# Second chunk's and sample rows' embedding products at experts 20 to 22 instead of before and in experts 0 and 1

## The reference

```
x1 = LN1(alpha*x + W_out [pool_group(x) | mlstm_group(x)])
x2 = LN2(alpha*x1 + MoE(x1))            # top 4 of 32 experts, clamped SwiGLU
y  = x2 + sigmoid(x2 W_pg) * (p W_ple)  # gated per-layer input embedding
```

## Time and profile before

| | |
|---|---|
| median of 3 runs | 1104.46 us (1104.17 to 1105.55) |
| profiled execution | 1105.6 us, its span 1103.8 us |
| PE busy | 1077.7 us (98%), 5616 instructions |
| DVE busy | 436.8 us (40%) |
| ACT busy | 159.5 us (14%) |
| DMA | 440.69 MB, mean 399 GB/s |

### The profile page before, as it was taken

One profiled execution on the slowest core, in us unless ns is written; L12 is line 12 of the kernel. 1 busy time (PEld: TensorE's weight loads), 2 busy tenths in 40 slices (PEclk: granted clock), 3 DMA queues, 4 the chain that ended last, 5 costly groups with the idle time before them and its releaser, 6 DMA issues.

```text
span 1103.8 us, 14800 instructions
## 1 busy us (share of the span) xinstructions
PE 1077.7 (98%) x5616; PEld 425.9 (39%) x5616; DVE 436.8 (40%) x1109; ACT 159.5 (14%) x306; POOL 78.9 (7%) x107
## 2 busy tenths in 40 slices
PE   9999999999999999999999999999999999999998
PEld 7786433333333333333333333333333333333344
DVE  1648663333333333333333333333333333333345
ACT  1532341100000000000000000000000000000033
POOL 0747420000000000000000000000000000000000
PEclk9999999999999999999999999999999999999999
DMA  9989989999999999999999999999999999999961
GB/s 319 267 313 399 287 352 395 428 436 428 429 432 435 423 433 433 433 427 435 433 429 432 433 433 427 432 433 433 428 433 435 426 431 433 432 423 428 425 243 40
DMA packets 41027, 440.69 MB, mean 399 GB/s; under 512 B 8816, under 2 KB 16236, under 8 KB 25653
## 3 DMA queue, kind: packets, MB, share of 16 engines
q1 hardware_dynamic: 39945, 439.00, 95.4%
q0 software_dynamic: 368, 0.57, 0.2%
q10 hardware_dynamic: 676, 0.59, 0.2%
HBM read 436.61 MB, written 3.77 MB: 399 GB/s over the span
## 4 chain that ended last, share of the span: by engine, by line
PE 65%; DMA 20%; DVE 9%; issue 2%; POOL 2%; ACT 1%; DVEq 0%; SPq 0%; ACTq 0%; POOLq 0%
PE bank L1024 27%; DMA ring<-in_w_mlp 19%; PE bank L1104 16%; PE bank L971 4%; PE bank L605 3%; DVE proj L1663 3%; PE bank L1184 3%; PE bank L784 3%; DVE proj L1660 2%; DVE proj L1658 2%; PE bank L1085 1%; PE bank L984 1%; POOL ring L2141 1%; PE bank L1019 1%; PE bank L977 1%
## 5 line engine op out<-in xcount | busy, mean ns | idle before, releaser
L1024 PE MATMUL bank<-ring,proj 128*64 128x512 f32 x2024 | 461.5, 597 | 9.0 <-DMA ring<-in_w_mlp 9.0
L1624 DVE SCALAR_TENSOR_TENSOR xT<-bank,proj,xT 128x512 f32<-128x512 f32 x128 | 90.2, 746 | 428.3 <-PE bank L971 427.1
L1024 PEld LDWEIGHTS bank<-ring,proj 128*64 128x64 f32 x2024 | 137.6, 136 | 288.9 <-issue 263.0
L1104 PE MATMUL bank<-ring,pool_side 128*64 128x512 f32 x1024 | 226.8, 595 | 0.4 <-ACT pool_side L1993 0.4
L1104 PEld LDWEIGHTS bank<-ring,pool_side 128*64 128x64 f32 x1024 | 71.7, 137 | 133.3 <-issue 130.4
L1987 ACT ACTIVATE proj<-proj 128x256 f32<-128x256 f32 x64 | 26.7, 417 | 527.5 <-DVE proj L1657 527.5
L1615 DVE TENSOR_SCALAR proj<-bank,ln_rows_of_fours 128x64 f32<-128x64 f32 x256 | 67.4, 335 | 24.8 <-PE bank L984 24.8
L971 PE MATMUL bank<-mixT 64*128 64x512 f32 x264 | 74.5, 641 | 0.5 <-ACT mixT L1996 0.5
L605 PE MATMUL bank<-xT,ring 128*128 128x264 f32 x320 | 74.3, 388 | 0.3 <-ACT proj L1809 0.3
L605 PEld LDWEIGHTS bank<-xT,ring 128*128 128x128 f32 x320 | 59.9, 190 | 12.3 <-issue 1.6
L950 PE MATMUL bank<-xreg,proj 128*64 128x512 f32 x248 | 58.5, 592 | 0.0
(11 more groups left out here) (371 smaller groups left out, 634.6 us busy)
## 6 DMA issues: line engine op xcount, KB each, us to landing
ring<-in_w_mlp SPq DMA_DIRECT2D x77, 4096.0 KB, 27.6
ring<-in_w_mlp SPq DMA_DIRECT2D x36, 2048.0 KB, 14.9
ring<-in_w_in SPq DMA_DIRECT2D x9, 1024.0 KB, 14.9
ring<-in_w_out SPq DMA_DIRECT2D x4, 1024.0 KB, 8.8
ring<-in_w_ple_gate SPq DMA_DIRECT2D x4, 1024.0 KB, 26.9
xreg<-in_x_prompt SPq DMA_DIRECT2D x4, 512.0 KB, 4.1
ring<-q_row SPq DMA_DIRECT2D x1, 2048.0 KB, 7.0
ring<-k_row SPq DMA_DIRECT2D x1, 2048.0 KB, 7.3
```

Of the source, the lines that this page charges most:

```text
L1024: last = pe.matmul(first_bank(t, q), xgT[:, k % 4, k // 4, :], first_columns(rows_, t, q), start=False, stop=(k == KD - 1))
L1104: last = pe.matmul(bank[4][BLOCK * h:BLOCK * (h + 1), :], aT[:, m, BLOCK * t:BLOCK * (t + 1)], w[:, k % 2, 512 * h:512 * h + 512], start=F ...
L1624: ins = STT(total[:, c, s], ins_bank[h][:, :], gate_table[:, c, bass.ds(n, 1)], total[:, c, s], ALU.mult, ALU.add)
```

## The change

Half 0 of chunk 1's embedding moves to expert 20, half 1 to expert 21 (k = 0 behind the product k = 1, k = 1 behind the product k = 3), the sample rows' to expert 22 (behind k = 5). Both halves now use bank 3. In the two places before expert 0 where half 0 was computed, PE does `keep_dense(4)` and `keep_dense(2)` on bank 7. Experts 20 to 23 are written out on PE (`middle`); ACT's loop ends before expert 20. `late[1]` is no longer filled by SP: ACT issues this DMA in expert 22, behind its copy of the sample rows' embedding and ahead of that expert's sigmoid.

```diff
-        EMBED_BANKS = {0: (bank[1], bank[6]), 1: (bank[7], bank[3]), 2: (bank[5],)}
+        EMBED_BANKS = {0: (bank[1], bank[6]), 1: (bank[3], bank[3]), 2: (bank[5],)}
...
                 load_next(n)
-                if n == SLOTS + 18:
-                    sp.wait_ge(sem("ple_ps"), 3)
-                    load_late(1)
...
-            def keep_dense(times):
+            def keep_dense(times, unread=bank[2]):
                 for _ in range(times):
-                    pe.matmul(bank[2][:, 0:P], ident, ident, start=True, stop=True)
+                    pe.matmul(unread[:, 0:P], ident, ident, start=True, stop=True)
...
             count_places(1, ()).then_inc(sem("pos_ps"), 1)
-            pe.wait_ge(sem("ple_in"), 16)
-            early_embedding(0, (0,))
+            keep_dense(4, bank[7])
...
-                    if opening and j == 0 and k in (1, 3):
-                        early_embedding(1, (k // 2,))
-                    if opening and j == 0 and k == 1:
-                        pe.wait_ge(sem("ple_done"), 1)
+                    if middle and j < 2 and k in (1, 3):
+                        if (j, k) == (0, 1):
+                            pe.wait_ge(sem("ple_in"), 16)
+                        early_embedding(j, (k // 2,))
...
-                        if opening and j == 1:
-                            pe.wait_ge(sem("hotT_done"), 2)
+                        if middle and j == 2:
+                            pe.wait_ge(sem("hotT_done"), n + 1)
                             early_samples()
-                if opening and j < 2:
-                    pe.wait_ge(sem("ple_done"), j + 2)
+                if middle and j < 3:
+                    pe.wait_ge(sem("ple_done"), j + 1)
...
             spread_places(0)
-            early_embedding(0, (1,))
+            keep_dense(2, bank[7])
...
-            with pe.Fori(STEP, npass * EXPERTS - 2 * STEP, STEP) as n:
+            with pe.Fori(STEP, npass * EXPERTS - 3 * STEP, STEP) as n:
                 for j in range(STEP):
                     expert(n + j, j)
+            for j in range(STEP):
+                expert(npass * EXPERTS - 3 * STEP + j, j, middle=True)
...
-            embedded_early(0)
             act.nop().then_inc(sem("out_done"), 1)
...
-            for j in range(STEP):
-                if j == 0:
-                    embedded_early(1)
-                elif j == 1:
+            with act.Fori(0, npass * EXPERTS - 3 * STEP, STEP) as n:
+                for j in range(STEP):
+                    expert(n + j, j)
+            for j in range(2 * STEP):
+                if j < 2:
+                    embedded_early(j)
+                elif j == 2:
                     act.wait_ge(sem("ple_ps"), 3)
                     act.copy(embedded_samples, EMBED_BANKS[2][0][:, 0:256]).then_inc(sem("ple_done"), 1)
-                expert(j, j)
-            with act.Fori(STEP, npass * EXPERTS - STEP, STEP) as n:
-                for j in range(STEP):
-                    expert(n + j, j)
+                    act.dma_start(late[1], unit_weights(EXPERTS - 2 * STEP, 1)).then_inc(sem("late_in"), 16)
+                expert(npass * EXPERTS - 3 * STEP + j, j % STEP)
```

More of the change, by code:

```diff
@@ L1009, in first_bank, with expert @@
                 return bank[q][BLOCK * t:BLOCK * (t + 1), :].rearrange("p (x i) -> p x i", i=8)
-            def expert(n, j, closing=0, opening=False):
+            def expert(n, j, closing=0, opening=False, middle=False):
                 i4 = n - j
```

## The result

| | median | range | runs |
|---|---|---|---|
| before | 1104.95 us | 1104.17 to 1105.55 | 9 |
| after | 1108.22 us | 1105.41 to 1110.94 | 9 |

The ratio is 1.003, 95% interval 1.0021 to 1.0038: 3.3 us slower, outside the forecast range of 1102.8 to 1106.5 us, and slower by more than the 0.2% that the prediction set as the border of no change. Eight of the nine runs after have a mean granted clock of 0.997 or 0.998 of full speed; the ninth has 1.000, and took 1105.41 us. The profiled execution took 1108.37 us, its span 1106.6 us, mean clock 0.998.

A forecast was written before the change was run, and what follows sets the result against it. Loads set the pace, with 1.16 us of PE cover at expert 29's k = 4 quad. Stream -0.1, holes 0, late[1] 0, middle products 0: profiled 1105.6 becomes 1105.5, median 1104.4 us, range 1102.8 to 1106.5.

The forecast's parts named there:

- Clock (slower, 0.07): Rival, chance 0.07: clock falls to 1.2 GHz behind expert 0's new hole; stream moves 3.6 us, time 1108.0.
- The hole: Expert 0 without its two product pairs: PE waits 2.3 us for DVE before the second combine; their 2.1 us return nothing.
- The load that stood at 175.29: Load behind expert 0's second layer, last held back by slot release: the stream shifts with it, 0.1 us earlier.
- late[1] 0 (moved inside the same stream): Loads behind its early place come 2.43 us sooner; sent at about 791 it takes 2.43 us back: 0 in the sum.
- 0 to 1.5 us, if a part of the sixteen engines runs dry: Bounds for holes in the stream, closest at the first quad (landed 250.2), with late[1] no longer early; 0 taken.
- Written-out code: The new middle experts are written out, as those that gave PE's 27.99 us per expert; the sum has no term for it.
- The start's shift: Before expert 0, keep_dense(4) takes 1.28 us where early_embedding took 0.96: gather_chunk(1) starts 0.32 us later.
- The middle: Experts 20 to 22: the 5.2 us of products are swallowed, 2.4 by the earlier stream, 3.4 by slower loads; cost 0.
- The ring: Sign: the stream of loads is 2.4 us ahead of before up to expert 22.
- Expert 24: Opens at 834.1 as before, with 1.8 us of cover left.
- the last wait: Expert 29's k = 4 quad, at 984.41 in before, near 984.3 after; its landing sets the end.
- The rival of extra room on a second queue: Faster, chance 0.07: ACT's queue brings late[1] without slowing SP's loads, the stream keeps 2.43 us; time 1102.0.

The follow-up runs named there:

- e1: The changed kernel with sixteen matmuls nobody reads (keep_dense(8)) in PE's wait behind product k = 3 of expert 0: 1106.59 us, ratio 1.0019.
- e2: The changed kernel with eight matmuls nobody reads (keep_dense(4)) in PE's wait in expert 0, half the hole left: 1106.61 us, ratio 1.0014.
- e9: The kernel of e1 (hole in expert 0 filled) without the load of late[1], 1 MB left out: 1104.37 us, ratio 0.9989 to the kernel before.
- e3: The kernel before without half 1's two product pairs of chunk 1's embedding in expert 0, nothing in their place: 1104.98 us, ratio 1.000.
- e7: The kernel before with the changed start alone: keep_dense(4) and (2) before expert 0, chunk 1's embedding left out, late[1] early: 1106.07 us, ratio 1.0004.
- e8: The code of e4 with late[1] issued by ACT in expert 22 instead of early by SP, no product moved: 1108.09 us, ratio 1.0025.
- e10: The kernel before without SP's load of late[1], 1 MB left out, nothing else changed: 1104.79 us, ratio 0.9989.
- e4: The kernel before with experts 20 to 23 written out on PE and 20 to 27 on ACT, nothing moved: 1106.27 us, ratio 1.0012.
- e5: The changed kernel with the hole filled as in e1 and late[1] issued by SP, ahead of expert 24's single unit, instead of ACT: 1107.66 us, ratio 1.0022.
- e6: The code of e4 with the six products done a second time in experts 20 to 22, results unread, late[1] early: 1106.68 us, ratio 1.0011.

## Why the prediction was wrong

Two steps failed, the clock and `late[1]`. Filling the hole returned 1.2 to 1.8 us of the 3.3 (e1, e2); taking the load of `late[1]` out as well removed all of the rest (e9). The intervals of after and of each filled kernel overlap, but eight of nine runs after lie above 1107.3 us, and seven of the 22 of e1 and e2.

**"Clock (slower, 0.07)" was given too small a chance.** The hole was forecast at 2.3 us and measured 2.16, its place and its uselessness were right (e3: no gain), and the fall was described as a rival, with PEclk dipping as its sign. I let it stand at 0.07 because no row of before showed a fall. But no row of before shows such a hole either: the earlier trace rows end at 0.7 us, and the longest in the whole trace is 1.47 us at the very start, with a clock of 1.00 behind it. So the rows said nothing about 2.3 us in either direction. With 8 of 9 runs after and 9 of 11 of e7 at the lower mean clock, it was the likely course. Its price was over-sized, 3.6 us forecast; the trace shows 1.70 in the pair of products. The clock was back to 0.97 in the window behind it, so less than one pair ran slow. The load that stood at 175.29 was issued at 177.4, 2.1 us later (0.9 of it this execution's late start), where the forecast was within 0.3. What a fall costs at the end is less sure: e7, which has it in the kernel before, is 0.4 us slower by the ratio, with no change inside the interval.

**"late[1] 0 (moved inside the same stream)" was wrong.** The step assumed that 2.43 us of loads are worth 2.43 us wherever they stand. At its late place the unit is paid in full in the stream: the landings from 796 to 805 slip by 2.5 us in after, by 2.1 in e1, 2.4 in e2 and 1.7 in e8. That opens a wait of 1.56 us at 808 (after) or 2.17 at 807 (e1), the latter with a second fall of the clock. In the whole time the late load costs 3.3 us (e1 against e9, 2.4 by the medians), the early one 1.2 (e10, 0.7 by the medians; the interval of its ratio runs from 0.2 to 2.1 us). The move alone costs 1.4 to 1.8 us (e8 against e4), with the fall of the clock at 807 that all ten runs of e8 bear the sign of.

Why the early unit costs less than its 2.43 us isn't shown. The landings of before and e10 alone suggest that the lead shrinks at the first quad: -1.1 at 216, +0.4 at 250. But with the start taken off, the six kernels without the early load and without a fall at 160 (e1, e2, e5, e8, e9, e10) are 1.7 to 3.2 us ahead of before at 216, 1.3 to 2.5 at 250 and 1.7 to 3.0 at 708, while those with the early load and no fall (e4, e6) are 0.1 to 0.6 ahead: some of the lead may go at 250, and most of it is there again at 708. So the bound of the prediction, "0 to 1.5 us, if a part of the sixteen engines runs dry", is neither confirmed nor excluded.

**Written-out code was costed at nothing,** and that may be a third step that failed. e4, which changes nothing else, is 1.0 us slower by the medians and 1.3 by the ratio, while e9, which has the same code, is not slower than e10, which has not. So what the filled kernel e1 still loses goes with the load at its late place, but how much of it the code adds while that load is there isn't known.

The other steps. The start's shift was smaller than summed: in the timeline the gather begins 1.07 us behind the eight small products and began 1.04 behind the pair that they replace (143.29 to 144.33), so it came 0.03 us later by the change, not 0.32. The middle: no waits from expert 20's k = 4 to 22's end, first wait at expert 16's k = 4 (610.61), then again at 23, all as forecast, and e6 confirms that the products are swallowed. The ring was to be 2.4 us ahead up to expert 22; it was 0.6 ahead. Of what is missing, 0.9 us is this execution's late start, which no step could foresee, and the rest is of the size of the fall: with the start taken off, e3 and e7, which have a fall and the early load, are 1.0 and 1.1 us behind before at 216, and after is 1.4 ahead, where the six kernels without early load and fall are 1.7 to 3.2 ahead. Expert 24 was to open at 834 and opened at 837.35; the last wait was to be near 984.3 and is 987.16. The rival of extra room on a second queue fell clearly: the rate stays at 430 GB/s between 700 and 830 us, and `late[1]` pushed expert 23's quad back by about its own 2.43 us. The Trainium skill, page "Trainium Kernel Development and Optimization", Key Constraints, says that DMAs issued from these queues run on the same 16 DMA engines and interleave; this trace agrees, with 430 GB/s before and beside `late[1]`.

**Open.** In all eight profiles with experts 20 to 23 written out the landings slip 0.5 to 1.8 us between 708 and 796 us, and in none of the other three (e3, e7, e10). The DMA view of that stretch shows what is new beside the loads, of after:

```profile
DMA packets 2142, 55.96 MB, mean 430 GB/s; under 512 B 239, under 2 KB 239, under 8 KB 239
...
q8 instruction: 5, 0.08, 0.3%
```

where before has no packet on that queue. But 0.08 MB at this rate are 0.2 us, less than the slip. Whether the fetches make the slip, and whether it costs anything at the end, isn't settled. e5's median is 1.1 us above e1's, with intervals of the ratio that overlap; its landings make the same steps (-1.0 to +0.6 by 796, to +3.0 behind `late[1]`), so no difference between the two queues is shown. A version that keeps the products early as cover and beats the kernel before wasn't found; e9 and e10, the only ones below it, leave a load out.

## What to carry to other kernels

Work that fills an engine's wait is free where it stands, and taking it away can cost: of a new hole in TensorE ask what the clock does behind it, and if no row shows a hole of that length, give it an even chance, not a small one. Don't take a load that is moved inside a saturated stream to be free. Here the same megabyte cost 0.7 to 1.2 us of the whole time early, where the consumer had a full ring ahead of it, and 2.4 to 3.3 us late, where every quad was waited for or soon would be; on SP's queue it cost no less than on ACT's. Ask where the wait that it opens will stand, and what the clock does behind it.

## What the runs showed of the hardware

- A single hole in PE's work of 2.15 or 2.16 us was followed by a granted clock of 0.60 or 0.61 over the next 4 us in the profiles, and by a mean clock of 0.997 or 0.998 in 17 of 20 runs (after, e7). With the 4.06 us of e8 all ten runs were at 0.997 or 0.998.
- The length of the hole alone doesn't tell. In the profiles the clock fell behind holes of 1.87 us (e3, with 0.998 in 3 of its 11 runs), 1.98 (e2) and 2.17 (e1), and stayed at 1.00 behind 2.05 us (e5, at 977), 1.56 (after, at 808) and 1.05 (e2).
- In each of the six profiles with a fall (after, e1, e2, e3, e7, e8) the pair of products behind the hole took 5.35 us instead of 3.65, whether the hole was 1.87 us or 4.06.
- A DMA of 1 MB issued on ACT's queue at 791.95 landed at 808.4, in 16.5 us, while SP's quads, with 29 us of transfers queued, take 30 us. It passed the quad that SP had issued at 786.1, which landed at 818.3. The rate stayed at 430 GB/s, and the landings on SP's queue slipped by 2.5 us between 796 and 805.
